# Normalising the rows of the step in front before the maximum of the present step, in both softmax attentions

## The reference

```python
# first block, forgetting attention (block of 128 queries)
logits = einsum('bqhd,bkhd->bhqk', qb, k) * scale + cq[..., None] - cum[:, :, None, :]
logits = where(mask, logits, neg)
p = softmax(logits, axis=-1);  out = einsum('bhqk,bkhd->bqhd', p, v)
# first block, chunked attention: the same with bias = rel_table[:, rel]
# second block, window with meta tokens and a sink
p = softmax(concatenate([s_meta, s_band, s_sink], axis=-1), axis=-1)
of = einsum(p[..., :N_META], vm) + einsum(p[..., N_META:N_META + NB], vb)
```

## Time and profile before

| | us |
|---|---|
| runs, median (3 runs, 2090.93 to 2095.31) | 2094.03 |
| profiled execution, device time | 2093.15 |
| its span, first to last instruction | 2091.3 |
| TensorE busy | 1983.7 (95%) |
| VectorE busy | 1005.7 (48%) |
| ScalarE busy | 727.0 (35%) |

### The profile page before, as it was taken

How to read it: one execution, slowest core, us unless ns; L and a number is a source line. 1 busy time by engine, 2 the same in 40 slices (tenths; PEclk the granted TensorE clock), 3 DMA queues, 4 the chain that set the end, 5 groups by cost and what they waited for, 6 DMA issues and landing times.

```text
span 2091.3 us, 26797 instructions
## 1 busy us (share of the span) xinstructions
PE 1983.7 (95%) x10909; PEld 1671.3 (80%) x10909; DVE 1005.7 (48%) x1364; ACT 727.0 (35%) x972; POOL 23.8 (1%) x45
## 2 busy tenths in 40 slices
PE   5899999997999999979999999899999999999997
PEld 2787887873888888769999999687888878888885
DVE  7688753436455542264443322667323454444323
ACT  2454444324445532152222212455333332222111
POOL 0100000000000000000000000000000000000000
PEclk9999999998999999999999999999999999999999
DMA  6644212220222222212222222211112222222221
GB/s 269 215 158 134 99 61 102 102 99 20 81 97 83 100 83 97 102 39 82 100 80 94 72 95 92 73 61 42 61 61 81 102 81 99 100 100 74 97 90 61
DMA packets 34847, 195.45 MB, mean 93 GB/s; under 512 B 3680, under 2 KB 3696, under 8 KB 19552
## 3 DMA queue, kind: packets, MB, share of 16 engines
q1 hardware_dynamic: 29008, 173.55, 23.6%
q0 software_dynamic: 5776, 21.02, 3.1%
HBM read 192.46 MB, written 2.10 MB: 93 GB/s over the span
## 4 chain that ended last, share of the span: by engine, by line
PE 88%; DVE 8%; ACT 2%; issue 1%; DMA 1%; SPq 0%; DVEq 0%; ACTq 0%
PE PS L600 86%; DVE W_lo L1625 2%; DVE INV L1669 1%; DMA A_low<-in_wada 1%; PE PS L756 1%; ACT W_hi L1184 1%; DVE N L1674 1%; DVE A_high L2103 1%; DMA ring<-in_wada 0%; DVE ring L2103 0%; DVE RS L1646 0%; DVE PT_lo L1707 0%; DVE stats L1692 0%; DVE X L2135 0%; DVE stats L1856 0%
## 5 line engine op out<-in xcount | busy, mean ns | idle before, releaser
L600 PE MATMUL PS<-H_hi,W_hi 128*128 128x512 f32 (+1 forms) x1976 | 632.2, 354 | 48.8 <-DVE H_lo L1657 19.4
L600 PE MATMUL PS<-H_hi,W_lo 128*128 128x512 f32 (+1 forms) x1976 | 632.9, 354 | 0.0
L600 PE MATMUL PS<-H_lo,W_hi 128*128 128x512 f32 (+1 forms) x1976 | 632.0, 354 | 0.0
L1625 DVE TENSOR_TENSOR W_lo<-W_raw,W_hi 128x2048 fp32r<-128x2048 f32 (+2 forms) x170 | 352.9, 2076 | 311.6 <-ACT W_hi L1184 311.0
L600 PEld LDWEIGHTS PS<-H_hi,W_hi 128*128 128x128 f32 x1976 | 350.0, 191 | 106.6 <-issue 42.8
L1184 ACT ACTIVATE W_hi<-W_raw 128x2048 fp32r<-128x2048 f32 (+2 forms) x170 | 295.6, 1739 | 325.4 <-PE PS L600 324.6
L600 PEld LDWEIGHTS PS<-H_lo,W_hi 128*128 128x128 f32 x1976 | 349.3, 191 | 50.6 <-issue 0.2
L600 PEld LDWEIGHTS PS<-H_hi,W_lo 128*128 128x128 f32 x1976 | 349.1, 191 | 49.9 <-issue 0.2
L600 PE MATMUL PS<-G_hi,W_lo 128*128 128x512 f32 (+1 forms) x704 | 210.2, 339 | 0.0
L600 PE MATMUL PS<-G_hi,W_hi 128*128 128x512 f32 (+1 forms) x704 | 209.6, 338 | 0.0
L600 PE MATMUL PS<-G_lo,W_hi 128*128 128x512 f32 (+1 forms) x704 | 209.3, 338 | 0.0
(11 more groups left out here) (246 smaller groups left out, 2045.2 us busy)
## 6 DMA issues: line engine op xcount, KB each, us to landing
W_raw<-in_wts SPq DMA_DIRECT2D x119, 1024.0 KB, 4.8
W_raw<-in_wdown SPq DMA_DIRECT2D x48, 704.0 KB, 4.1
ring<-in_wada POOLq DMA_DIRECT2D x32, 512.0 KB, 3.8
A_high<-in_wada SPq DMA_DIRECT2D x6, 1024.0 KB, 18.0
A_low<-in_wada SPq DMA_DIRECT2D x2, 1024.0 KB, 10.5
X<-in_xT SPq DMA_DIRECT2D x2, 1024.0 KB, 10.0
X<-in_xT POOLq DMA_DIRECT2D x1, 2048.0 KB, 8.8
out<-N SPq DMA_DIRECT2D x8, 256.0 KB, 2.1
```

Of the source, the lines that this page charges most:

```text
L600: return nc.tensor.matmul(*a, **kw)
L1625: vector.tensor_tensor(W_lo[:, c.odd, 0:size], W_raw[:, c.odd, 0:size], W_hi[:, c.odd, 0:size].bitcast(FP32), ALU.subtract).then_inc(w_lo, 1)
```

## The change

In `front_steps` and `win_steps` of VectorE the part for unit t-1 (reciprocal and scaling) is put ahead of the part for unit t (maximum). The part for t-2 stays behind both. All waits and semaphores stay the same; the other engines' programs are unchanged.

```diff
             def front_steps():
                 for t in range(UNITS + 7):
-                    if t < UNITS:
-                        w = P * (unit(t)[4] + 1)
-                        dve.wait_ge(sem("f_scores"), t + 1)
-                        vector.tensor_reduce(fstat[:, 0, t:t + 1], score_bank(t)[:, 0:w], AX.X, ALU.max, negate=True
-                                             ).then_inc(sem("f_max"), 1)
                     u = t - 1
                     if 0 <= u < UNITS:
                         w = P * (unit(u)[4] + 1)
...
                         vector.tensor_scalar(PR[:, u % 3, 0:w], PR[:, u % 3, 0:w], fstat[:, 2, u:u + 1], None, ALU.mult
                                              ).then_inc(sem("f_normed"), 1)
+                    if t < UNITS:
+                        w = P * (unit(t)[4] + 1)
+                        dve.wait_ge(sem("f_scores"), t + 1)
+                        vector.tensor_reduce(fstat[:, 0, t:t + 1], score_bank(t)[:, 0:w], AX.X, ALU.max, negate=True
+                                             ).then_inc(sem("f_max"), 1)
                     u = t - 2
```

More of the change, by code:

```diff
@@ L1852, in win_steps @@
                         back_values()
[L1853 to L1860, removed]
                     u = t - 1
@@ L1872, in win_steps @@
                                              ).then_inc(sem("att_normed"), 1)
+                    if t < WIN_UNITS:
+                        _, h, _, _, i = win_unit(t)
+                        dve.wait_ge(sem("att_scores"), t + 1)
+                        vector.tensor_reduce(stat[:, 3, t:t + 1], score_bank(t)[:, 0:win_width(i)], AX.X, ALU.max
+                                             ).then_inc(sem("att_key_max"), 1)
+                        dve.wait_ge(sem("att_key_max"), t + 1)
+                        vector.tensor_scalar(stat[:, 0, t:t + 1], stat[:, 3, t:t + 1], vec("sinks", h), -1.0,
+                                             ALU.max, ALU.mult).then_inc(sem("att_max"), 1)
                     u = t - 2
```

## The result

The changed kernel takes 2102.07 us (median of 8 runs, 2097.13 to 2105.12) against 2092.89 (8 runs, 2090.93 to 2095.31): ratio 1.0039, interval 1.0027 to 1.0052. It is 0.4% slower, twice what a measurement can tell from no change, and outside the range that was forecast (2092.5 to 2100.5). Forecast was plus 2.1 us, measured is plus 9.2; that before's median is now 1.1 lower than the three runs gave makes part of the distance between 2096.1 and 2102.07, but not most of it. The span of its profiled execution is 2099.6 us, 8.3 more than before; TensorE again holds most of the chain that ended last.

A forecast was written before the change was run, and what follows sets the result against it. TensorE was taken as the bound, so only its gaps in the two attentions counted: plus 1.9 us in the first block and 0.2 in the windowed attention, plus 2.1, median 2096.1 us, range 2092.5 to 2100.5.

The forecast's parts named there:

- The first pair: Start of the first block's attention: Exp of unit 1 starts later, TensorE's 1.60 us wait grows; plus 0.87 us.
- The place at 171.73: First block, Exp of unit 23: the moved normalisation delays a chain without idle time; plus 0.53 us.
- that at 288.33: First block, Exp of unit 55: it ends too close to the next scores to hide the block; plus 0.48 us.
- The two waits of 0.2 us: First block, step of the values: TensorE's two short waits for PT_lo go; minus 0.4 us.
- the third step's 0.46: First block, Exp of unit 3: it comes later by the whole normalisation block; plus 0.46 us.
- The windowed attention: All terms there: 0.85 us of costs less 0.62 of shorter waits for PT_lo; plus 0.2 us.
- The wait before unit 4: Windowed attention at 1375.12: TensorE's 1.44 us wait for Exp of unit 3 grows; plus 0.33 us.
- those at phases 1 and 3: Windowed attention, waits ahead of the values at 1387.59 and a head pair later: plus 0.28 and plus 0.24 us.
- six pairs said to have 0.41 to 0.53 us between Exp and scores: Windowed attention: ScalarE's copies hold the odd Exp, so the block costs TensorE 0; without that cover up to 0.35 us each.
- the first rival: Both attentions: the odd Exp becomes the bound at all 17 close pairs; about plus 7, 2101 us; chance 0.18.
- the third rival: The forecast sum and one fall of TensorE's clock more; plus 3.7, 2097.8 us; chance 0.10.
- The second: Rival: earlier normalisation shortens TensorE's waits for PT_lo more than counted; about minus 3, 2091 us; chance 0.06.

The follow-up runs named there:

- e6: The changed kernel with 35 useless matmuls where TensorE waits in the windowed attention (ahead of unit 4's scores and of the values); 2095.01 us, ratio 1.0006.
- e9: The kernel before the change, with the same useless matmuls in the windowed attention as e6; 2093.64 us, ratio 0.9997.
- e7: The kernel before the change, with useless VectorE reductions in the windowed attention so that TensorE's waits are about the changed kernel's; 2100.20 us, ratio 1.0034.
- e11: The kernel before the change, with 98 useless matmuls in nearly all of TensorE's longer waits in both attentions; 2090.78 us, ratio 0.9987.
- e1: The new order in the first block's forgetting and band attention alone, the windowed attention as before; 2095.53 us, ratio 1.0011.
- e2: The new order in the windowed attention alone, the first block as before; 2101.72 us, ratio 1.0043.
- e5: The changed kernel measured again, nothing altered, on another chip run; 2103.83 us, ratio 1.0038.
- e3: The new order in even steps alone of both attentions, odd steps as before the change; 2094.29 us, ratio 1.0001.

## Why the prediction was wrong

**The waits of the first block came out nearly as worked out.** The first pair: the end of Exp of unit 1 was 1.04 us behind the start of the first maximum (95.58 to 96.62); the changed kernel's timeline has

```profile
96.41 0.29 DVE L1700 TENSOR_REDUCE stats<-PS 128x1 f32<-128x128 f32 x1
97.42 0.29 DVE L1695 TENSOR_SCALAR PR<-PR,stats 128x128 f32<-128x128 f32 x1
97.94 0.37 ACT L1184 ACTIVATE PR<-PS,stats 128x128 f32<-128x128 f32 x1 [0.75 <-DVE stats L1700]
98.45 0.38 PE L600 MATMUL PS<-KH,QH 64*128 64x256 f32 x2 [2.55 <-ACT PR L1184]
```

96.41 to 98.31, 1.90 us: plus 0.86 (0.87 forecast), and the wait went from 1.60 to 2.55. The place at 171.73 and that at 288.33 now read

```profile
175.04 0.33 PE L600 MATMUL PS<-KH,QH 64*128 64x128 f32 x2 [1.41 <-ACT PR L1184]
291.89 0.33 PE L600 MATMUL PS<-KH,QH 64*128 64x128 f32 x2 [0.41 <-ACT PR L1184]
```

plus 0.52 (0.53) and a new 0.41 (0.48). The two waits of 0.2 us are gone (minus 0.44). One term did not come: the third step's 0.46, since TensorE had been at the low clock just before, from 99.5 to 102.9 us, and reached the scores after Exp (105.30, against the end of Exp at 104.18). The sum is 0.86 + 0.52 + 0.41 - 0.44 = 1.35 where 1.9 stood. The idle time of the stretch agrees: 9.82 - 8.65 = 1.17 us more; the other 1.66 of its 2.83 are work at the low clock.

**The windowed attention** was forecast at plus 0.2. It grew by 4.54 us, 3.47 of them slower work with three falls more than before, and 1.07 idle time. So its waits were put too low as well: those listed went from 7.6 to 9.4 us. The wait before unit 4 went from 1.44 to 2.04, of which 0.33 was forecast. The savings did not show as shorter waits for the values, which come once in a phase of four units: those at phases 1 and 3 grew to 0.96 and 1.02 from 0.52 and 0.58 (0.28 and 0.24 forecast, so 0.2 too little each), and phase 2 stayed at 0.93. With the same filling in both orders the difference is 0.77 us (94.33 in e6, with one fall; 93.56 in e9, with none). In both attentions together idle time grew by 2.2 us, where the sum said 2.1. That is luck: it is 1.2 and 1.1, and 1.9 and 0.2 were forecast.

One reading was off without bearing on the sum: of the six pairs said to have 0.41 to 0.53 us between Exp and scores five do, the sixth has 0.70. And the first rival counts 17 close pairs but prices 14; the three left out, with 0.65 to 0.70 us, would have lost under 0.1 each.

**The step that failed** is the clock, which the sum of plus 2.1 puts at nothing. I had named the mechanism, but only as the third rival, "My sum, and one fall of the clock more", with its price from the one fall of before (1.6 us, against 1.2 to 1.7 measured), one occurrence and a chance of 0.10. There were four more in the profiled execution, one in the first block and three in the windowed attention: 1.66 + 3.47 = 5.1 us of slower work and 2.2 of waiting, 7.4 of the span's 8.3 us; the other 0.9 lies outside the two stretches (0.73 of it ahead of the first scores). I had looked for what speaks against it, the longest wait of before (2.4 us), behind which no fall follows, and gave more falls little weight. The row that spoke for it was the earlier trace rows itself. In front of it stands

```profile
1416.86 0.38 PE L600 MATMUL PS<-PTM_hi,VW 16*128 16x256 f32 x1 [0.58 <-DVE PTM_lo L1881]
```

a wait of 0.58 us ahead of the values, at a place that recurs with every phase. The Trainium skill, page "TensorE: Matmul & The Clock Gate", part 1 on the clock gate, says that activity releases the throttle and idling brings it back. By e6, e7 and e11 the trace agrees in sum, though not wait by wait: filling the waits held the clock at 1.00 where it had been 0.89, and making them longer lost it, with the falls behind waits of 0.85 to 1.24 us in e7.

**What is shown and what isn't.** Shown: nearly all of the loss lies in the windowed attention (e1, e2); waits of that size without the new order bring two thirds of it (e7, 6.2 of 9.2 us in the median); with the new order and the waits filled it is gone (e6). At which waits the clock falls is not settled. The same wait of 2.4 us near 1460 us is followed by no fall in before and in the changed kernel's first profile, and by a long one in e2 and e5; 0.93 us ahead of the values is followed by none in before (1404.8) and by one in the changed kernel (1411.6); and 2.0 us ahead of unit 4 by none in e7. So the length of the one wait doesn't decide it alone. The first rival, the odd Exp as the bound at all close pairs, is out: five waits for Exp in the first block where nine pairs were close, and two in the windowed attention as before. The second as well: the waits for PT_lo went from 5.0 to 4.4 us and not further.

## What to carry to other kernels

Where TensorE is nearly always busy, a list of its waits prices a reordering only while its clock holds. A stretch's busy time, set beside that of the same work in before, shows at once how much of a loss is not waiting. Ask of each wait that becomes longer how thin TensorE's work is around it, and look for a row below 1.0 at that place in the profile before; here one fall was a warning for every repetition of the pattern, and wanted to be priced that many times. And before a wait that can't be removed, useless matmuls into a free bank are worth a trial: in e11 they cost nothing that shows (220.83 us against 220.70 in the first block, 93.48 against 94.18 in the windowed attention), and the whole came to minus 0.13%.

## What had not been expected of the hardware

- Adding work made the kernel faster: 35 useless matmuls, some 0.12 us each from start to start, gave 8.8 us back (e6 against e5).
- A delay of VectorE of under 2 us in all cost 6.2 us of 2094 (e7), and its runs spread from 2097.5 to 2103.0.
- The falls account for part of the spread of runs that looks like noise. Of e3's eleven runs the four with a mean granted clock of 0.983 took 2090.5 to 2092.7 us, the seven with 0.980 to 0.982 took 2093.8 to 2096.1. In e11, at 0.982 to 0.986, the fastest run was 2087.84 us, the slowest 2093.05, the latter under the median of before's runs beside it, 2093.19.
